# Other places in VectorE's order for seven low parts and two bias additions between attention heads

## The reference

```python
proj = rmsnorm(h, norm_mix[layer]) @ w_in[layer]
gate_b, gate_c, u, c_q, c_kv_full, gate_logits = jnp.split(proj, split_at, axis=-1)
y_a = short_conv_mixer(gate_b, gate_c, u, conv_w[layer], w_conv_out[layer])
y_b = mla_mixer(c_q, c_kv_full, cos, sin, g_q, g_kv, w_uq, w_ukv, w_o)
g_a, g_b = jnp.split(jax.nn.sigmoid(gate_logits + b_gate[layer]), 2, axis=-1)
h = h + (g_a * y_a + g_b * y_b) @ w_mix_out[layer]
...
# per head and block of 128 queries
s = (q_nope @ k_nope.T + q_rope @ k_rope.T) * scale
s = where(k_chunk <= q_chunk, s, -inf)
p = softmax(s)
o = p @ v
```

## Time and profile before

| | |
|---|---|
| median of 3 runs | 1139.03 us (1138.82 to 1139.06) |
| profiled execution: time, span | 1138.38 us, 1136.7 us |
| mean granted clock of TensorE | 0.998 of full speed |
| busy share: PE, PEld, DVE, ACT, POOL | 98%, 82%, 76%, 66%, 3% |
| chain that ended last, share of the span | PE 77%, DVE 18%, ACT 2%, issue 2%, DMA 1% |

### The profile page before, as it was taken

How to read it: one execution, slowest core, us unless ns; L and a number is a source line. 1 busy time by engine, 2 the same in 40 slices (tenths; PEclk the granted TensorE clock), 3 DMA queues, 4 the chain that set the end, 5 groups by cost and what they waited for, 6 DMA issues and landing times.

```text
span 1136.7 us, 15525 instructions
## 1 busy us (share of the span) xinstructions
PE 1109.6 (98%) x5470; PEld 929.4 (82%) x5470; DVE 867.9 (76%) x1031; ACT 755.5 (66%) x941; POOL 35.1 (3%) x64
## 2 busy tenths in 40 slices
PE   9999999999999999999999999999999999999997
PEld 8888777888888888888777888887778887888885
DVE  6568666765554456468666779999999899999997
ACT  6555767455344345556667456799987898988785
POOL 3001000000000001001001000000000000000000
PEclk9999999999999999999999999999999999999999
DMA  8745523668555354646534648999999999999993
GB/s 321 280 147 185 174 92 109 218 216 304 184 185 185 111 184 139 218 132 189 171 103 138 199 169 282 390 401 412 415 418 366 382 404 408 406 415 400 417 371 143
DMA packets 120553, 294.94 MB, mean 259 GB/s; under 512 B 9007, under 2 KB 33677, under 8 KB 119965
## 3 DMA queue, kind: packets, MB, share of 16 engines
q1 hardware_dynamic: 119072, 288.23, 69.9%
q0 software_dynamic: 960, 5.28, 1.2%
q10 hardware_dynamic: 444, 0.47, 0.1%
HBM read 292.90 MB, written 1.05 MB: 259 GB/s over the span
## 4 chain that ended last, share of the span: by engine, by line
PE 77%; DVE 18%; ACT 2%; issue 2%; DMA 1%; ACTq 0%; DVEq 0%
PE bank L1739 22%; PE bank L1741 21%; PE bank L1740 21%; DVE w_lo L1514 10%; DVE w_lo_more L1514 3%; PE bank L2152 2%; PE bank L2153 2%; PE bank L1783 1%; PE bank L1955 1%; PE bank L1971 1%; PE bank L1963 1%; ACT w_hi L961 1%; DVE w_lo L1182 1%; PE bank L2135 1%; DVE hid_buf L1653 1%
## 5 line engine op out<-in xcount | busy, mean ns | idle before, releaser
L1182 DVE TENSOR_TENSOR w_lo<-raw,w_hi 128x1024 fp32r<-128x1024 f32 (+4 forms) x141 | 240.5, 1710 | 139.1 <-ACT w_hi L736 138.7
L736 ACT ACTIVATE w_hi<-raw 128x1024 fp32r<-128x1024 f32 (+5 forms) x141 | 201.4, 1432 | 151.8 <-PE bank L1741 151.8
L1514 DVE TENSOR_TENSOR w_lo<-raw,w_hi 128x1792 fp32r<-128x1792 f32 (+3 forms) x148 | 286.5, 1965 | 10.1 <-ACT w_hi L961 9.4
L961 ACT ACTIVATE w_hi<-raw 128x1792 fp32r<-128x1792 f32 (+3 forms) x148 | 244.0, 1668 | 43.0 <-PE bank L1741 31.1
L1739 PE MATMUL bank<-w_hi,aT_hi 128*128 128x512 f32 (+1 forms) x592 | 235.5, 398 | 0.6 <-DVE w_lo L1310 0.5
L1741 PE MATMUL bank<-w_hi,aT_lo 128*128 128x512 f32 (+1 forms) x592 | 229.6, 388 | 0.0
L1740 PE MATMUL bank<-w_lo,aT_hi 128*128 128x512 f32 (+1 forms) x592 | 229.6, 388 | 0.0
L1739 PEld LDWEIGHTS bank<-w_hi,aT_hi 128*128 128x128 f32 x592 | 111.2, 188 | 24.2 <-issue 3.2
L1741 PEld LDWEIGHTS bank<-w_hi,aT_lo 128*128 128x128 f32 x592 | 111.2, 188 | 22.8
L1740 PEld LDWEIGHTS bank<-w_lo,aT_hi 128*128 128x128 f32 x592 | 111.3, 188 | 20.2
L1514 DVE TENSOR_TENSOR w_lo_more<-raw,w_hi_more 128x1792 fp32r<-128x1792 f32 (+3 forms) x50 | 96.7, 1941 | 4.6 <-ACT w_hi_more L961 4.6
(11 more groups left out here) (328 smaller groups left out, 1787.9 us busy)
## 6 DMA issues: line engine op xcount, KB each, us to landing
raw<-in_moe_w_gate SPq DMA_DIRECT2D x128, 448.0 KB, 6.5
raw<-in_moe_w_up SPq DMA_DIRECT2D x128, 448.0 KB, 6.4
raw<-in_moe_w_down SPq DMA_DIRECT2D x112, 512.0 KB, 6.5
raw<-in_w_in SPq DMA_DIRECT2D x40, 768.0 KB, 4.4
raw<-in_dense_w_gate SPq DMA_DIRECT2D x22, 512.0 KB, 3.8
raw<-in_dense_w_up SPq DMA_DIRECT2D x22, 512.0 KB, 4.6
raw<-in_dense_w_down SPq DMA_DIRECT2D x11, 1024.0 KB, 4.9
raw<-in_w_in SPq DMA_DIRECT2D x20, 512.0 KB, 4.8
```

Source lines behind the costliest of these rows:

```text
L736: act.activation(dst, src, ACT.Copy).then_inc(hi_made[j], 1)
L961: act.activation(split_of(hi_slot, m), raw_of(i, n), ACT.Copy).then_inc(e_hi_made, 1)
L1182: dve.tensor_tensor(dst, src, high, ALU.subtract).then_inc(lo_made[j], 1)
L1514: dve.tensor_tensor(split_of(lo_slot, m), raw_of(i, n), split_of(hi_slot, m).bitcast(F32), ALU.subtract).then_inc(e_lo_made, 1)
```

## The change

VectorE's low parts of the granules get a table of their own, LOW_PART_AT, and stand in slots 3, 6, 7, 9, 12, 13 and 17 instead of 3, 5, 7, 9, 11, 13 and 15, and there between the division and the maximum instead of behind the maximum. The bias additions stand in slots 8 and 14 instead of 6 and 12, also between division and maximum instead of at the slot's end. What ScalarE and TensorE do, and in which order, is not changed; the table GRANULE_AHEAD still sets the high parts. Lines behind the change get numbers that are higher by 3 to 8.

```diff
--- before.py
+++ after.py
@@ -106,6 +106,9 @@
 
 GRANULE_AHEAD = {6 * g + s: (BLK_GATE + g + 1, j) for g in range(2) for s, j in ((2, 0), (4, 1), (6, 2))}
 GRANULE_AHEAD.update({14: (BLK_CONV1, 0), HEADS + 2: (BLK_CONV1, 1)})
+LOW_PART_AT = {6 * g + s: (BLK_GATE + g + 1, j) for g in range(2) for s, j in ((3, 0), (6, 1), (7, 2))}
+LOW_PART_AT.update({HEADS + 1: (BLK_CONV1, 0), HEADS + 2: (BLK_CONV1, 1)})
+BIAS_AT = {8: 1, 14: 2}
 
 
 PAIR_CU, PAIR_B, PAIR_GATE0, PAIR_UQ, PAIR_UKV, PAIR_CONV, PAIR_GATE, PAIR_CONV1, PAIR_ATT, PAIR_MIX, PAIRS = (
@@ -1412,6 +1415,11 @@
                         link(dve.reciprocal(row_inv, row_sum))
                         dve.tensor_scalar(p_buf[:, 0:P], p_buf[:, 0:P], row_inv[:, 0:1], None, ALU.mult).then_inc(p_scaled, 1)
                         dve.tensor_scalar(p_buf[:, P:3 * P], p_buf[:, P:3 * P], row_inv[:, 1:2], None, ALU.mult).then_inc(p_scaled, 1)
+                    if n in LOW_PART_AT and n <= HEADS + 1:
+                        b, j = LOW_PART_AT[n]
+                        lo(B + b, j, SLAB_SIZES[j])
+                    if n in BIAS_AT:
+                        add_bias(BIAS_AT[n])
                     if 1 <= n <= HEADS:
                         dve.wait_ge(s_made, HEADS * L + n)
                         if n >= 2:
@@ -1420,18 +1428,13 @@
                             dve.tensor_tensor_reduce(out=s_buf[:, keys_part], in0=bank[B_S][:, keys_part], in1=mask[:, keys_part],
                                                      scale=-SCALE, scalar=-MASKED, op0=ALU.add, op1=ALU.min,
                                                      accum_out=neg_max[:, t:t + 1]).then_inc(max_made, 1)
-                        if n - 1 in GRANULE_AHEAD:
-                            b, j = GRANULE_AHEAD[n - 1]
-                            lo(B + b, j, SLAB_SIZES[j])
                     if n >= 4 and n % 2 == 0:
                         dve.wait_ge(o_made, head_pairs(L, n // 2 - 1))
                         dve.tensor_copy(oT[:, n // 2 - 2, :], bank[B_O][:, 0:S]).then_inc(o_in, 1)
                     if n == HEADS + 2:
                         attended_lo(4 * L + 1, (0, 1))
-                    if n in (GATE_SLOTS, 2 * GATE_SLOTS):
-                        add_bias(n // GATE_SLOTS)
                     if n == HEADS + 2:
-                        b, j = GRANULE_AHEAD[n]
+                        b, j = LOW_PART_AT[n]
                         lo(B + b, j, SLAB_SIZES[j])
                 add_bias(3)
                 lo(B + BLK_CONV1, 2, SLAB_SIZES[2])
```

## The result

| | before | after |
|---|---|---|
| median (lowest to highest), 8 runs each | 1139.06 us (1138.45 to 1139.97) | 1142.16 us (1141.85 to 1143.17) |
| profiled execution: time, span | 1138.38, 1136.7 us | 1142.60, 1140.9 us |
| mean granted clock of TensorE | 0.998 | 0.998 |

After stands to before as 1.0028 (95% interval 1.0019 to 1.0037), which is 3.1 us slower; the forecast was 1142.6 and slower.

The account below looks back on a forecast made before the run. TensorE, busy 98% of the span, was taken as the bound, its transposes waiting for VectorE's division. Two layers at +1.79 gave +3.6 us, 1142.0 profiled, plus 0.65 for the median: 1142.6, range 1140.8 to 1143.8.

Parts of the forecast that it names:

- the prediction's D: TensorE's delay against before at layer 0's transposes: +0.31 at slot 4, +1.81 at slot 14, +1.79 at slot 16.
- the sum: Heads' delay of 1.79 us in each of two layers, +3.6 us, taking the profiled execution from 1138.38 to 1142.0.
- the last step of the sum: Layer 0's heads: late high part and query copy put slot 15's exponential at 182.35; delay +1.79 at slot 16.
- The faster one: Heads: high parts are ready when low parts ask, today's holds end, 4.0 us in all, 1135.0; chance 0.05.
- Its second clause: VectorE in the heads: the ready maximum passes the waiting low part, with a time of about 1135.0.
- The half-swallowed rival: Experts' stage: transfers set its pace, layer 1's delay vanishes, +1.8 remains, 1140.8; chance 0.13, shared with smaller chains.
- The bounds: Heads' three chains each off by 0.2, 0.6 per layer: 2.4 to 4.8, 1141.4 to 1143.8; later transfers cost nothing.
- The holds that it would clear: VectorE holding up TensorE in the heads: 0.53 in slots 4, 10, 16 and 0.20 in 7, 13; 1.99 per layer.

Follow-up runs that it names:

- the last two kernels: Change with low parts behind the maximum in roomier slots, bias additions ending slots 8, 16: 1135.42; that plus earlier high parts 0 and a gate-logits chunk moved to slot 2: 1134.84.
- low parts alone: The changed kernel with its bias additions put back at the ends of slots 6 and 12: 1141.32 us, 1.0018 of before.

## Why the prediction was right

**What held, step by step.** Delays of TensorE at the transposes, the prediction's D beside after's rows less before's less 0.08:

| slot | 4 | 7 | 8 | 10 | 13 | 14 | 16 |
|---|---|---|---|---|---|---|---|
| predicted | 0.31 | 0.11 | 0.76 | 1.36 | 1.16 | 1.81 | 1.79 |
| measured | 0.32 | 0.14 | 0.78 | 1.37 | 1.16 | 1.82 | 1.57 |

The start-to-start distances carried the whole chain to slot 14 within 0.03, so up to there the forecast is right by its mechanism and not by luck. That the profiled execution took 1142.60, the forecast's own figure, is luck: the sum gave 1142.0 for a profiled execution, and the heads added 3.2 us, not 3.6. The rest came behind VectorE's last instruction (last section). The wait of slot 7 went and slots 8 and 14 got new ones, as said; the bias additions ran from 154.00 to 155.32 (153.90 to 155.22 and the start); the experts' stage and its waits stayed.

**The mis-sized term** is the last step of the sum, the exponential of slot 15. The prediction put the high part "from 180.50 to 181.97" and then the query copy's 0.38, for a start at 182.35, or 182.43 with this trace's start. It started at 182.22. Both instructions were counted with their recorded length, although what follows on the same engine starts earlier: ScalarE's rows show 1.37 from the high part to the copy (recorded 1.47) and 0.27 from the copy to the exponential (recorded 0.37). That is 0.2 too much per layer, 0.4 of the two layers' 3.6, and the sum with the measured distances is 3.2. The same 0.2 us is why the next stage's low part gave back 0.25 where the prediction let the late exponential eat all of it, and it is the larger part of why slot 16's wait fell from 0.68 to 0.29 where it was to stay. The rest of that, and slot 10's wait of 1.05 by the prediction's count instead of 1.2, come from some 0.15 us that TensorE had lost in each case before it reached the scores. So the waits at the transposes came to 6.5 us and not to about 7. An instruction of another engine that waits for the result does wait for the recorded end: the low part started 0.03 after it. The Trainium skill, "Perfetto Trace Analysis", section "Optimizing Scalar/DVE Operations", says that an instruction's write acknowledgement, at its end, overlaps with the next instruction; these rows agree, with 0.10 us.

**The rivals.** The faster one was right about the mechanism: with the high parts ready the same order of VectorE gives 1135.96, 1.0 above its 1135.0; of this 1.0, slot 16 makes 0.6, since it returns only 0.25 us of its 0.53 in each layer. It was rightly refused for this change by the one row that showed ScalarE's high part ending at 135.31. Its second clause, a ready maximum that passes the waiting low part, did not belong there: by the prediction's own figures the low part starts at 135.34, before the maximum is ready at 136.17, so overtaking would have changed nothing. Nor is it true that no row of before has a ready instruction behind a waiting one. Slot 3 has one: its high part was made at 135.31, VectorE stood idle until 136.17 for the maximum's scores, and the low part, which waits for nothing but its high part, started only behind the maximum, at 136.73. The Trainium skill's page "TensorE: Matmul & The Clock Gate" (opening table) has VectorE's queue as strictly first in, first out; these rows agree, with 0.86 us for which a ready instruction didn't pass a waiting one.

The half-swallowed rival fell: +1.63 of layer 1 arrives whole at the last instruction. The bounds had the later transfers cost nothing because their granules are read only after the heads; that reason is not right, since the next stage's granule 0 gets its high part in slot 14, but the conclusion is: that high part starts in after without a wait in layer 0 (180.58), and the delay behind the heads is the delay in them.

The Trainium skill's "Perfetto Trace Analysis", Optimization Strategies, would have the engines optimized that block TensorE; read as the prediction read it, as speaking for the change, it had the wrong sign here and the right one for the last two kernels (−3.5 and −4.1 us). The holds that it would clear were the right ones; what the change put in their place was a wait for an engine that wasn't ready.

## What to carry to other kernels

Work that only fills an engine's idle time belongs where its input is already made and where the gap up to the next instruction of the critical chain is longer than the work; both are read from the timeline, slot by slot. Either condition alone was not enough: slot 3 of after had the room and no input, slot 7 of "low parts alone" the input and no room. Placed ahead of such an instruction and fed by another engine one step too late, it makes that engine's delay part of the chain: the same order of VectorE cost 3.1 us with the high parts late and gained 3.1 with them one slot earlier. When a chain is summed, use the distance from start to start for what follows on the same engine, and the recorded end for what waits on another.

## What the runs showed of the hardware

The time from VectorE's last instruction to the end of the span, in which the output is written, was 5.4 us in the profiled execution of before (1136.7 less 1131.29) and 6.3 in that of after (1140.9 less 1134.57), with nothing changed there; the seven other profiled executions lie between these two. So the spans of before and after differ by 4.2 us where the work differs by 3.3, and single executions shouldn't be compared by their spans to less than 1 us. The overlap of 0.1 us between a record's end and the next start on ScalarE is the same for 1536 columns as for a copy of 256; the prediction had used VectorE's distances (1.67 for a low part recorded with 1.75) and left it out here.
